# Squares summed on VectorE, up products two pairs ahead, a norm's scale and shift split, and a last stage by block

## The reference

```python
for i in range(2):                                   # first_block
    h = rms_norm(x, norm_mix_g[i])
    x = x + (dsa_mixer if i == 0 else retention_mixer)(h, ...)
    h = rms_norm(x, norm_ffn_g[i])
    u = causal_conv3(h @ w_up) + conv_b              # 1024 -> 2 * 2816
    x = x + (silu(u[:, :2816]) * u[:, 2816:]) @ w_down
mod = silu(c) @ w_ada + b_ada                        # second_block: six vectors of 1024
h = rmsnorm(x, norm_mix_w) * (1 + scale_m) + shift_m
x = x + gate_m * hybrid_mixer(h, ...)                # state-space scan in 4 groups, pooling
h = rmsnorm(x, norm_mlp_w) * (1 + scale_f) + shift_f
x = x + gate_f * (square(relu(h @ w_up_2)) @ w_down_2)   # 1024 -> 4096 -> 1024
return rmsnorm(x, norm_final_w)
```

## Time and profile before

| | before |
|---|---|
| median of 3 runs | 1263.19 us (1260.96 to 1263.36) |
| profiled execution | 1263.84 us, span of its instructions 1262.0 us |
| TensorE (PE) busy | 1208.2 us |
| VectorE (DVE) busy | 964.8 us |
| ScalarE (ACT) busy | 708.2 us |
| GpSimd (POOL) busy | 85.4 us |

### The profile page before, as it was taken

How to read it: one execution, slowest core, us unless ns; L and a number is a source line. 1 busy time by engine, 2 the same in 40 slices (tenths; PEclk the granted TensorE clock), 3 DMA queues, 4 the chain that set the end, 5 groups by cost and what they waited for, 6 DMA issues and landing times.

```text
span 1262.0 us, 25971 instructions
## 1 busy us (share of the span) xinstructions
PE 1208.2 (96%) x9260; PEld 1157.1 (92%) x9260; DVE 964.8 (76%) x1764; ACT 708.2 (56%) x1104; POOL 85.4 (7%) x104
## 2 busy tenths in 40 slices
PE   8989899999899999999999989999999999999996
PEld 7978899999899999999999978898898999899995
DVE  5766788888787897788888878988896557666665
ACT  5555655556454555465555657767775335645443
POOL 0002000000211111200000000011010002000001
PEclk9989899999999999999999989999999999999998
DMA  8334466666466866756565616455446455555550
GB/s 307 108 109 160 147 199 220 205 227 205 149 235 248 290 217 230 262 167 218 199 215 183 200 57 229 151 183 172 160 137 206 160 183 184 188 192 182 187 166 34
DMA packets 72462, 235.69 MB, mean 187 GB/s; under 512 B 7360, under 2 KB 15808, under 8 KB 72272
## 3 DMA queue, kind: packets, MB, share of 16 engines
q1 hardware_dynamic: 63728, 203.86, 48.1%
q0 software_dynamic: 8528, 30.98, 7.6%
q10 hardware_dynamic: 144, 0.02, 0.0%
HBM read 233.73 MB, written 1.09 MB: 186 GB/s over the span
## 4 chain that ended last, share of the span: by engine, by line
PE 71%; DVE 16%; issue 6%; ACT 5%; POOL 1%; DVEq 1%; DMA 0%; ACTq 0%; SPq 0%; PEldq 0%
PE ps L190 22%; PE ps L192 22%; PE ps L191 22%; DVE w_lo L182 6%; DVE arena L1738 2%; DVE arena L1009 1%; ACT w_hi L177 1%; DVE arena L1011 1%; DVE arena L1003 1%; ACT arena L952 1%; PE ps L1451 1%; POOL sq L243 0%; DMA w_raw<-stream 0%; ACT a_hi L317 0%; DVE b_lo L1032 0%
## 5 line engine op out<-in xcount | busy, mean ns | idle before, releaser
L190 PE MATMUL ps<-a_hi,w_hi 128*128 128x256 f32 x1656 | 479.6, 290 | 7.4 <-DVE a_lo L1320 2.6
L182 DVE TENSOR_TENSOR w_lo<-w_raw,w_hi 128x1024 fp32r<-128x1024 f32 x381 | 463.9, 1224 | 17.8 <-ACT w_hi L177 13.8
L191 PE MATMUL ps<-a_lo,w_hi 128*128 128x256 f32 x1656 | 470.6, 284 | 0.0
L192 PE MATMUL ps<-a_hi,w_lo 128*128 128x256 f32 x1656 | 470.4, 284 | 0.0
L177 ACT ACTIVATE w_hi<-w_raw 128x1024 fp32r<-128x1024 f32 x381 | 391.0, 1048 | 25.2 <-PE ps L192 21.2
L190 PEld LDWEIGHTS ps<-a_hi,w_hi 128*128 128x128 f32 x1656 | 319.3, 193 | 16.8 <-issue 9.1
L191 PEld LDWEIGHTS ps<-a_lo,w_hi 128*128 128x128 f32 x1656 | 319.8, 193 | 0.5 <-issue 0.2
L192 PEld LDWEIGHTS ps<-a_hi,w_lo 128*128 128x128 f32 x1656 | 319.6, 193 | 0.0
L190 PE MATMUL ps<-b_hi,w_hi 128*128 128x256 f32 x672 | 193.5, 288 | 9.0 <-issue 5.7
L191 PE MATMUL ps<-b_lo,w_hi 128*128 128x256 f32 x672 | 191.5, 285 | 0.0
L192 PE MATMUL ps<-b_hi,w_lo 128*128 128x256 f32 x672 | 191.5, 285 | 0.0
(11 more groups left out here) (290 smaller groups left out, 1470.9 us busy)
## 6 DMA issues: line engine op xcount, KB each, us to landing
w_raw<-stream SPq DMA_DIRECT2D x381, 512.0 KB, 4.0
arena<-ada POOLq DMA_DIRECT2D x48, 512.0 KB, 4.9
c_hi<-cum_rows POOLq DMA_DIRECT2D x4, 1024.0 KB, 7.6
con<-consts SPq DMA_DIRECT2D x1, 1440.0 KB, 11.3
arena<-x SPq DMA_DIRECT2D x2, 512.0 KB, 4.4
arena<-row_cols POOLq DMA_DIRECT2D x2, 512.0 KB, 5.0
out<-arena SPq DMA_DIRECT2D x4, 256.0 KB, 2.4
arena<-c_rows POOLq DMA_DIRECT2D x1, 512.0 KB, 4.0
```

The costliest lines, as they stand in the source:

```text
L182: dve.tensor_tensor(w_lo[:, s % RING], w_raw[:, s % RING], w_hi[:, s % RING].bitcast(F32), ALU.subtract).then_inc(w_lo_ready, 1)
L190: pe.matmul(o, wh, xh, start=start, stop=False, skip_group_check=shared)
L191: pe.matmul(o, wh, xl, start=False, stop=False, skip_group_check=shared)
L192: return pe.matmul(o, wl, xh, start=False, stop=stop, skip_group_check=shared)
```

## The change

Five things are changed.

1. All adds of squares go from GpSimd to VectorE. `add_pairs` stands in the first feed-forward behind a split of VectorE's first pair, and at the head of `retention_vec`; `add_tile` behind each tile of the output products; `add_four` at piece 10 of a head, and in the tail of a group. GpSimd is left with DMA issues.
2. The feed-forward's up pairs run two pairs ahead of the down products (order up 0, up 1, up 2, down 0, up 3, down 1, ...), with four operand slots. The slabs are loaded and split in that order; the splits of the last pair's slabs stand behind its operand. A SiLU of one column (`table_probe`) stands in front of the copy of `inv`.
3. The state-space norm: ScalarE multiplies `res` by the scale before the factor is known (`gained`), VectorE multiplies by `inv` in place two tiles ahead, ScalarE adds the shift and rounds in one pass, VectorE adds the shift again and subtracts.
4. MLP start: the four turns stand together behind the sums, into banks 0 to 3.
5. MLP end: the last four slabs by block; a fourth operand slot for the last tile; VectorE does the final multiplies in place of GpSimd, block by block.

The diff, cut to its core ("..." marks what is left out):

```diff
+        def add_squares(dve, i, j, n, base):
+
+            dve.wait_ge(sq_added, base)
+            dve.tensor_tensor(sq[:, i:i + n].rearrange("p m t -> p (m t)"), sq[:, i:i + n].rearrange("p m t -> p (m t)"),
+                              sq[:, j:j + n].rearrange("p m t -> p (m t)"), ALU.add).then_inc(sq_added, 1)
...
+        def add_pairs(dve, v):
 
             first = ADDED[v] - 4
...
-            pool.tensor_tensor(sq[:, 0], sq[:, 0], sq[:, 1], ALU.add).then_inc(sq_added, 1)
...
+            dve.wait_ge(sq_ready, NT * v + 8)
+            add_squares(dve, 0, 2, 2, first)
+            add_squares(dve, 4, 6, 2, first)
+            add_squares(dve, 0, 4, 2, first + 2)
+            add_squares(dve, 0, 1, 1, first + 3)
+
+        def add_tile(dve, v, m):
+
+            dve.wait_ge(sq_ready, NT * v + m + 1)
+            if m:
+                add_squares(dve, 0, m, 1, ADDED[v] - NT + m)
+
+        def add_four(dve, n, per, it):
+
+            for i, width in enumerate((2, 1)):
+                dve.wait_ge(sq_added, val(n + i, it, per))
+                dve.tensor_tensor(sq[:, 0:width].rearrange("p m t -> p (m t)"), sq[:, 0:width].rearrange("p m t -> p (m t)"),
+                                  sq[:, width:2 * width].rearrange("p m t -> p (m t)"), ALU.add).then_inc(sq_added, 1)
...
+                    add_tile(dve, v, m - 1)
             vec_prep(dve, v, NT - 1, g)
+            add_tile(dve, v, NT - 1)
...
+        def down_order(p):
+
+            return 3 * p + 6 if p < FF_PAIRS - 2 else 2 * FF_PAIRS + p
...
                 pe.wait_ge(f["operand"], val(p + 1, it, UNROLL))
-                down_slab(pe, s, b_hi[:, p % 2], b_lo[:, p % 2], p == 0, p == FF_PAIRS - 1, it, ds)
...
             pe.wait_ge(inv_ready, v)
-            down(0, s0 + 4)
+            up_pair(2)
+            down(0)
             with pe.Fori(0, LATER) as it:
                 for u in range(UNROLL):
-                    up_pair(2 + u, s0 + 5 + 3 * u, it, 3 * UNROLL)
-                    down(1 + u, s0 + 7 + 3 * u, it, 3 * UNROLL)
-            for p in range(2 + UNROLL * LATER, FF_PAIRS - 2):
-                up_pair(p, s0 + 3 * p - 1)
-                down(p - 1, s0 + 3 * p + 1)
-            up_pair(FF_PAIRS - 2, s0 + 3 * FF_PAIRS - 7)
-            up_pair(FF_PAIRS - 1, s0 + 3 * FF_PAIRS - 5)
-            for n in (3, 2, 1):
-                down(FF_PAIRS - n, s0 + 3 * FF_PAIRS - n)
+                    up_pair(3 + u, it)
+                    down(1 + u, it)
+            for p in range(3 + UNROLL * LATER, FF_PAIRS):
+                up_pair(p)
+                down(p - 2)
+            down(FF_PAIRS - 2)
+            down(FF_PAIRS - 1)
...
+            def pair(p, it=None):
+                s, ds = pair_at(s0, p), 0 if it is None else 3 * UNROLL
                 hi_ahead(act, s + 4, it, ds)
+                if p < FF_PAIRS - 1:
+                    hi_ahead(act, s + 5, it, ds)
                 if p == 0:
-                    act_inv(act, v)
-                hi_ahead(act, s + 5, it, ds)
+                    act_root(act, RS[v], NB)
+                    act.activation(table_probe[:, 5 + L:6 + L], ident[:, 0:1], ACT.Silu).then_inc(act_step, 1)
+                    spread_copy(act, v)
                 tap(p, 0, it)
-                if p:
+                if 2 <= p < FF_PAIRS - 1:
                     hi_ahead(act, s + 6, it, ds)
                 tap(p, 1, it)
                 silu(p, it)
...
+                if p == FF_PAIRS - 1:
+                    for n in range(5, 9):
+                        hi_ahead(act, s + n)
...
                 lo_ahead(dve, s + 3, it, ds)
                 if p == 0:
+                    if L == 0:
+                        add_pairs(dve, v)
+                    lo_ahead(dve, s + 4)
                     vec_inv(dve, step, v, EPS_A)
                     dve.wait_ge(inv_ready, v)
-                used = s - 1 if p == FF_PAIRS - 1 else s
-                evict(p, 0, used, it, ds)
-                lo_ahead(dve, s + 4, it, ds)
+                evict(p, 0, s, it, ds)
+                if p and not last:
+                    lo_ahead(dve, s + 4, it, ds)
                 taps(p, 0, it)
-                evict(p, 1, used, it, ds)
+                evict(p, 1, s, it, ds)
                 taps(p, 1, it)
                 dve.wait_ge(f["conv"], val(2 * p + 2, it, 2 * UNROLL))
                 dve.wait_ge(f["gate"], val(p + 1, it, UNROLL))
                 dve.tensor_tensor(glu[:, p % 2], gate[:, p % 2], conv[:, p % 2, 1], ALU.mult).then_inc(f["glu"], 1)
-                if p:
+                if p >= 2 and not last:
                     lo_ahead(dve, s + 5, it, ds)
                 dve.wait_ge(f["hi"], val(p + 1, it, UNROLL))
-                dve.tensor_tensor(b_lo[:, p % 2], glu[:, p % 2], b_hi[:, p % 2].bitcast(F32), ALU.subtract).then_inc(f["operand"], 1)
+                dve.tensor_tensor(b_lo[:, p % 4], glu[:, p % 2], b_hi[:, p % 4].bitcast(F32), ALU.subtract).then_inc(f["operand"], 1)
+                if last:
+                    for n in range(4, 8):
+                        lo_ahead(dve, s + n)
 
...
+            add_pairs(dve, 2)
...
+                    if j == 10:
+                        dve.wait_ge(ret_sq, per_head(2, 2, h, it))
+                        add_four(dve, ADDED_RET + 2 * h, 2, it)
...
+            def gain(m):
+                act.wait_ge(res_ready, NT * 4 + m + 1)
+                act.activation(gained[:, m], res[:, m], ACT.Copy, scale=eff_scale[:, 0, m:m + 1]).then_inc(gained_ready, 1)
+
+            act.wait_ge(mod_ready, 2)
+            for m in range(5):
+                gain(m)
+            act_root(act, RS[4], NB)
+            for m in range(5, NT):
+                gain(m)
+            spread_copy(act, 4)
             for m in range(NT):
-                n = NT * (v - 4) + m
-                act.wait_ge(scaled_ready, n + 1)
...
+            def scale(m):
+                dve.wait_ge(gained_ready, m + 1)
+                dve.tensor_tensor(gained[:, m], gained[:, m], inv[:, :], ALU.mult).then_inc(scaled_ready, 1)
...
+                dve.wait_ge(a_hi_ready, NT * 4 + m + 1)
+                dve.scalar_tensor_tensor(out=a_lo[:, m], in0=gained[:, m], scalar=mix_shift(m), in1=a_hi[:, m].bitcast(F32),
+                                         op0=ALU.add, op1=ALU.subtract).then_inc(a_ready, 1)
...
+                if j == 2:
+                    dve.wait_ge(ysq_ready, in_group(1, 1, g, it))
+                    add_four(dve, ADDED_SSD + 2 * g, 2, it)
...
+        def tile_of(n):
+            return 3 if n == MLP_TILES - 1 else n % 3
...
+                    mm = pe.transpose(ps[:, r, m * P:(m + 1) * P], res[:, 4 * half + m, b * P:(b + 1) * P], ident)
...
             sum_added(pe, 5)
+            for r in range(4):
+                turn_res(r)
             up_tile(1)
             spread_inv(pe, 5)
             up_tile(2)
+            pe.wait_ge(res_tok_ready, 4)
             down(0)
-            turn_res(0)
...
+            up_tile(MLP_TILES - 2)
+            up_tile(MLP_TILES - 1)
+            for n in range(MLP_TILES - 4, MLP_TILES):
                 pe.wait_ge(hidden_operand, n + 1)
                 slab_ready(pe, down_at(n))
                 down_block(n, 0)
-            for n in (MLP_TILES - 2, MLP_TILES - 1):
+            for n in range(MLP_TILES - 4, MLP_TILES):
                 down_block(n, 1)
...
+                end_square(b, 0)
+                end_square(b, 1)
+                act_root(act, RS_FINAL + b, 1)
+                act.wait_ge(end_scaled, b + 1)
                 act.wait_ge(end_inv, b + 1)
...
+            for b in range(NB):
+                end_sum(b, 0)
+                end_sum(b, 1)
+                dve.wait_ge(summed, 2 * b + 1)
+                dve.tensor_tensor(result[:, b, 0:512], res_tok[:, b, 0:512], final_row[:, 0:512], ALU.mult).then_inc(end_scaled, 1)
+                end_var(b)
+                rsqrt(dve, step, RS_FINAL + b, 1, inv_end[:, b:b + 1], done=end_inv)
+                dve.wait_ge(end_inv, b + 1)
+                dve.wait_ge(summed, 2 * b + 2)
+                dve.scalar_tensor_tensor(out=result[:, b, 512:DM], in0=res_tok[:, b, 512:DM], scalar=inv_end[:, b:b + 1], in1=final_row[:, 512:DM],
+                                         op0=ALU.mult, op1=ALU.mult).then_inc(half_1_ready, 1)
...
+            def source(s):
+
+                for s0 in (S_FFN0, S_FFN1):
+                    if 4 <= s - s0 < 3 * FF_PAIRS - 2:
+                        return s - 2 if (s - s0 - 4) % 3 == 2 else s + 1
+                return s
```

More of the change, by code:

```diff
@@ L1042, in ffn_vec @@
                 for u in range(UNROLL):
-                    pair(2 + u, s0 + 5 + 3 * u, it)
+                    pair(2 + u, it)
                     if u in LOOP_DOTS_AT:
@@ L1326, in mod_vec @@
-            low(NT - 1)
+                if m + 2 < NT:
+                    scale(m + 2)
+                low(m)
         GRP = 12
@@ L1924, in mlp_pe @@
                     down(n, it)
-            for n in (MLP_TILES - 2, MLP_TILES - 1):
```

(19 more changed lines are left out.)

235 lines of the change are left out of this document (73 added, 162 removed).

## The result

The changed kernel took 1255.27 us (median of five runs) beside 1263.19 us for the kernel before; the ratio of the two is 0.9941 (95% interval 0.9928 to 0.9955). It is faster by 7.9 us; forecast were 1259.2 us, 4.0 us less than before (the terms add up to 3.9), and a range of 1257.0 to 1263.0 us. One of the five runs took 2975.64 us, why isn't known, and is not in the ratio; the other four lie between 1254.85 and 1255.37 us.

What follows compares the result with a forecast made beforehand. TensorE, busy 96%, was taken as the bound, with VectorE's pairs a hidden second one in the feed-forward loop. Terms 2.6 + 0 + 0.9 - 3.5 + 2.5 + 1.4 = 3.9 us off 1263.19 gave 1259.2 us, range 1257.0 to 1263.0.

Steps and rivals of the forecast that it cites:

- the norm's term: Second feed-forward and state-space norm: first scaling at 730.7 us, last lower half at 736.8; gain 1.2 us, 0.9 taken.
- the end's: MLP end: with four slabs by block, last multiply 5.15 us after TensorE's last product T instead of 6.6; gain 1.4 us.
- what follows the last multiply: From the last multiply to the end of the span: the forecast sum has no term for it.
- rival C: State-space groups: the VectorE-GpSimd lock frees VectorE, so the 3.5 us are not paid; 1255.7 us, chance 0.07.
- State-space groups: The add pair stands in VectorE's chain and takes 1.17 us in each of three looped groups: 3.5 us lost.
- First feed-forward, start: First sums ready 0.7 us earlier, pair 1 1.8 us earlier; then VectorE paces the loop, about 1.4 us won by the last pair.
- 23 matmuls take what 58 would: TensorE's pace from 134 to 141 us, where the granted clock is 0.51, the lower of its levels.
- First feed-forward, end: Residual adds at 315.8 us, sums at 325.6, low clock from 328.5 gone; gain 3.3 us, 2.6 taken.
- Rival A: TensorE's clock takes more: new idles at five places bring two more drops in unhidden work; 1262.0 us, chance 0.2.
- Last stage: start: MLP start: four turns together behind the sums without copies between, up 5 at 1089.6 us instead of 1092.1; gain 2.5 us.

Runs made afterwards that it cites:

- the first run: The changed kernel with the adds of the four state-space groups back on GpSimd, all else as changed: 1251.62 us.
- the old order's runs: Both feed-forwards in the old order: from the changed kernel, without the probe, 1255.44 us; from the first run's kernel, with the probe kept, 1247.69 us.
- all adds back: The changed kernel with every add of squares back on GpSimd in its old place, final multiplies left on VectorE: 1258.78 us.
- two slabs: The changed kernel with only the last two slabs of the last stage by block, final work still on VectorE: 1258.0 us.

## Why the prediction was wrong, step by step

The direction and the mechanisms were right, the size was not: 7.9 us for 4.0. Four steps failed: the norm's term (0.9 us for 1.8 measured), the end's (1.4 for 2.1), what follows the last multiply (taken as nothing, 0.8 measured), and a stretch at the low clock that was not read (1.5 to 1.6 us). The total fell near the 1255.7 us of rival C by luck: its mechanism did not happen, the 3.5 us were paid.

**State-space groups: right.** 3.7 us for 3.5, and the first run takes them away alone. The period grew by 1.3 us for the 1.2 forecast (two adds, 1.14 us in the row, and the waits around them). The prediction set rival C aside because hardly one split is stretched; nine of the 381 are (1.34 to 1.78 us beside GpSimd's adds, seven of them at the end of retention), and other rows of the kernel before are too:

```profile
118.38 1.01 DVE L333 SCALAR_TENSOR_TENSOR a_lo<-res,par,a_hi 128x256 fp32r<-128x256 f32 x1
120.46 2.41 POOL L243 TENSOR_TENSOR sq<-sq 128x512 f32<-128x512 f32 x1 [1.35 <-ACT sq L319]
```

The first takes 0.48 us elsewhere and stands beside a GpSimd add. In the three looped groups GpSimd's adds stretch no VectorE row but one split, by 0.12 us; in the fourth they do (1.15 us for 0.16 at 920.91 us, a part of the row), and there it reaches no mark. On the rule of the Trainium skill (SBUF — State Buffer, SBUF: two separate sides) that VectorE and GpSimd exclude each other for a whole instruction, whichever starts first: the stretched rows agree with the exclusion, but the start in the profile does not tell who waits. GpSimd's add of 120.46 us starts 0.04 us ahead of the split of 120.50 us, and it is the add that grows, from 1.28 us. What the waiting costs depends on which of the two is on the path.

**First feed-forward, start: right in kind.** VectorE paces the loop, and the 4.3 us of idle with the low clock were hardly any time (at most 0.7 us), as the old order's runs show. The prediction's "23 matmuls take what 58 would" counts 2.3 us of idle as matmuls: the 23 were busy for 4.74 us. No term of the sum rests on it. The first sums came 1.1 us sooner behind the attention's end (forecast 0.7; their mark itself moves by up to a microsecond between profiles, with the attention). Some 0.2 us of the rest are the row at 118.38 us above: with GpSimd's adds gone it takes 0.48 us, TensorE waits 0.38 us for the next operand instead of 0.90, and VectorE comes to its split sooner. The probe was worth 0.7 us here as costed (0.8), and the load lay against its activation in every trace, wherever the activation waited for nothing else; the drain that the Trainium skill adds (ScalarE: Activation LUTs, What ACT_TABLE_LOAD costs) is seen in none of them.

**First feed-forward, end: right.** Residual adds at 315.34 us for 315.8, sums at 324.83 for 325.6. That the low clock behind them goes was forecast, but it was taken for a fixed 1.4 us (by its own row 1.2; the terms of the 3.3 us add up to 3.1). From sums to spread the kernel before took 4.9 us with the stretch and 3.4 without it, so it costs 1.5; it is there in one profile of before and not in the other. I took 2.6 us of 3.3 for fear of a new low clock, which did not come. Rival A had it the wrong way round: the new idles of 1.2 to 1.6 us brought no low clock, and old ones went. What the prediction did not separate is the order itself: by the run with the old order it costs 0.84 us here and 0.87 in the second feed-forward, and the stage's gain is that of the adds, the probe and the low clock that is gone.

**Second feed-forward and norm: the term was mis-sized.** The feed-forward lost 1.06 us (0.9 forecast). The first scaling stands where it was said (726.63 us, that is 730.5 in the old count, for 730.7). But the passes were compared from start to start before (8.23 us, 8.65 to the end) and to the end after: 6.1 us forecast, 5.94 measured (731.29 + 1.28 - 726.63). That is 0.4 us, and 0.3 more were held back for a low clock. The stage's gain is 1.8 us for 0.9.

**Pooling's product: a step that wasn't there.** 1.5 to 1.6 us came from a stretch at the low clock that the prediction had not read, because none of the changed work is near it. Why it is gone stays open.

**Last stage: start right** (2.4 us for 2.5). **End mis-sized:** last multiply at T + 4.55 us, not T + 5.15, so 2.1 us for 1.4. With four slabs by block 1.2 us hang on GpSimd's absence (the run put back one multiply a block, before there were two), and with VectorE's multiplies 2.7 us on the four slabs; neither part would have won the 2.1 us alone. And the stores were not costed at all: before, all four were issued together (from 1257.17 us on, 1.81 us for four); now two are out before the last product's end. Last multiply to the span's end is 0.8 us shorter. The issuing is not what was won, since the last store is issued 1.2 us behind the start of the last multiply in both. But it lands sooner, with two under way and not four, here before and after:

```profile
DMA to landing us min/median/max: 2.0/2.4/2.7
DMA to landing us min/median/max: 2.0/2.2/2.3
```

The last one of before takes the 2.7 us, that of after the 2.3. The other 0.4 us lie between the last landing and the span's end, and no view says why.

**The base.** The kernel before lies between 1260.8 and 1264.2 us, which the working did not turn into a range. Its two profiles differ by 2.8 us: 1.65 between the attention and retention's spread, where one has a stretch at 328 us more and the other half of that at 134, and 1.0 in when the attention ends. The three failed terms (norm 0.9, end 0.7, stores 0.8) and the unread stretch (1.5) make 3.9 us, the size of what was missing; that it fits so closely is partly luck, since the profiles' sums are 8.8 and 6.1 us. The first feed-forward's term lies within its scatter (3.8 and 2.2 around 2.6).

## What to carry to other kernels

Where one engine paces a loop, look at what its in-between work covers: moving a filler out of a wait costs the wait, and an idle or slow stretch of the other engine is nearly free (here at most 0.7 us of 3.4). Add work to the engine that is behind only where it waits; the same adds won 5.5 to 7.2 us in the norms and lost 3.7 in the groups' chain. Read the stores of the last microseconds and every low-clock stretch of the profile, also those away from the change, before summing.

## What the hardware showed

The granted clock's low stretches came and went between executions of one kernel: behind the same idle of about 2 us at 328 us there was one of 0.51 in one profile and 1.00 in the other. The length of the idle alone did not tell: one of 4.3 us ahead of the first down product had a low stretch behind it in three profiles, one of 3.54 us there had none. Idles of 1.5 and 1.6 us, 8 us apart, brought none in any kernel of the new order with the probe; one of 2.1 us at 125 us brought one once. What 3.4 us at the low clock cost hung on who was on the path: 1.5 us at 328 and at 953 us, and 0.2 us at 748 to 754 us, where three kernels had it (all adds back, two slabs, the final multiplies on GpSimd) and the first masked heads came 41.7 us behind the norm's spread for 41.5.

A VectorE add of 128x512 took 0.69 us alone and 1.26 to 1.35 beside a GpSimd multiply of the same size when both its operands lay in SBUF; an add with one operand in PSUM kept its 0.68 us beside the same multiply (at 1246.95 us in the run with the final multiplies on GpSimd). Beside two weight splits in a row it was GpSimd's add that grew, from 1.28 to 3.54 us, and at the end of retention it was the split, from 1.22 to 1.38 and 1.78 us.
